# Expert layer: 16 more tokens through fetched expert rows, 368 instead of 384 through the dense product

## The reference

```
q = (xb @ w_q).reshape(T, 8, 2, 128)                       # 8 heads, two halves
s = einsum('thpd,hpkd->thpk', q, sub_keys)                 # 128 keys per half
sv, si = top_k(s, 16)
cand = sv[:, :, 0, :, None] + sv[:, :, 1, None, :]         # 16 x 16 pairs
top_s, pos = top_k(cand, 16)
eidx = the pair's index, si_0 * 128 + si_1                 # one of 16384 experts
gate = softmax(top_s)
act = gelu(einsum('thkd,td->thk', expert_u[eidx], xb))
out = einsum('thk,thkd->td', gate * act, expert_v[eidx])
```

## Time and profile before

| | |
|---|---|
| timed, median of 3 | 2393.5 us |
| profiled execution, its own time | 2388.96 us |
| its span | 2387.6 us |
| TensorE busy over the span | 2278.5 us (95%) |
| VectorE | 1777.1 us (74%) |
| ScalarE | 1095.6 us (46%) |
| GpSimd | 574.4 us (24%) |
| DMA moved | 466.79 MB, 196 GB/s on average |

### The profile page before, as it was taken

One profiled execution on the slowest core, in us unless ns is written; L12 is line 12 of the kernel. 1 busy time (PEld: TensorE's weight loads), 2 busy tenths in 40 slices (PEclk: granted clock), 3 DMA queues, 4 the chain that ended last, 5 costly groups with the idle time before them and its releaser, 6 DMA issues.

```text
span 2387.6 us, 34419 instructions
## 1 busy us (share of the span) xinstructions
PE 2278.5 (95%) x12827; PEld 2012.0 (84%) x12827; DVE 1777.1 (74%) x3434; ACT 1095.6 (46%) x1956; POOL 574.4 (24%) x419
## 2 busy tenths in 40 slices
PE   7989999999999999999999998999888899999998
PEld 5768999999999999999999997688655577777766
DVE  7889869988899976888888886633577645477764
ACT  4232343333488863333333335422366623566662
POOL 4110357888722212222222211200000020000001
PEclk9999999999999999999999999999999999999998
DMA  6546558899989999999999992111100022100012
GB/s 259 186 159 221 194 181 287 310 311 316 324 278 335 330 330 335 345 355 362 335 341 352 352 335 92 53 62 62 36 1 1 18 62 84 40 23 23 23 36 71
DMA packets 162374, 466.79 MB, mean 196 GB/s; under 512 B 15520, under 2 KB 72992, under 8 KB 159776
## 3 DMA queue, kind: packets, MB, share of 16 engines
q1 hardware_dynamic: 100512, 305.19, 36.0%
q0 software_dynamic: 36864, 134.23, 16.1%
q10 hardware_dynamic: 24832, 25.17, 3.3%
HBM read 412.10 MB, written 52.43 MB: 195 GB/s over the span
## 4 chain that ended last, share of the span: by engine, by line
PE 82%; DVE 7%; ACT 4%; issue 3%; DMA 3%; POOL 1%; SPq 0%; ACTq 0%; DVEq 0%; POOLq 0%
PE psum L491 7%; PE psum L629 7%; PE psum L492 7%; PE psum L493 7%; PE psum L631 7%; PE psum L630 7%; PE psum L482 6%; PE psum L483 6%; PE psum L484 6%; PE psum L602 4%; PE psum L509 2%; PE psum L978 2%; PE psum L795 2%; DMA arena<-hidden 2%; DVE weights_low L1536 1%
## 5 line engine op out<-in xcount | busy, mean ns | idle before, releaser
L1027 ACT ACTIVATE weights_high<-arena 128x1024 fp32r<-128x1024 f32 x355 | 374.6, 1056 | 462.5 <-PE psum L631 324.0
L1536 DVE TENSOR_TENSOR weights_low<-arena,weights_high 128x1024 fp32r<-128x1024 f32 x266 | 331.7, 1247 | 225.8 <-ACT weights_high L1027 224.6
L629 PE MATMUL psum<-hidden_high,weights_high 128*128 128x384 f32 x1024 | 344.0, 336 | 6.4 <-issue 3.7
L491 PE MATMUL psum<-x_high,weights_high 128*128 128x384 f32 x1024 | 345.8, 338 | 4.1 <-POOL weights_low L2186 2.7
L630 PE MATMUL psum<-hidden_low,weights_high 128*128 128x384 f32 x1024 | 342.7, 335 | 0.0
L631 PE MATMUL psum<-hidden_high,weights_low 128*128 128x384 f32 x1024 | 342.6, 335 | 0.0
L492 PE MATMUL psum<-x_low,weights_high 128*128 128x384 f32 x1024 | 342.2, 334 | 0.0
L493 PE MATMUL psum<-x_high,weights_low 128*128 128x384 f32 x1024 | 342.2, 334 | 0.0
L482 PE MATMUL psum<-x_high,weights_high 128*128 128x512 f32 x696 | 276.8, 398 | 14.0 <-DVE weights_low L1536 9.1
L484 PE MATMUL psum<-x_high,weights_low 128*128 128x512 f32 x696 | 272.4, 391 | 0.0
L483 PE MATMUL psum<-x_low,weights_high 128*128 128x512 f32 x696 | 272.4, 391 | 0.0
(11 more groups left out here) (263 smaller groups left out, 4294.4 us busy)
## 6 DMA issues: line engine op xcount, KB each, us to landing
arena<-in_stream SPq DMA_DIRECT2D x227, 512.0 KB, 4.6
arena<-in_v_rows SPq DMA_DIRECT2D x128, 512.0 KB, 6.4
arena<-in_ada_w SPq DMA_DIRECT2D x48, 512.0 KB, 3.5
hidden<-arena SPq DMA_DIRECT2D x128, 192.0 KB, 4.5
router<-arena SPq DMA_DIRECT2D x12, 2048.0 KB, 9.3
arena<-hidden SPq DMA_DIRECT2D x128, 192.0 KB, 6.8
arena<-router ACTq DMA_DIRECT2D x16, 1536.0 KB, 20.2
arena<-in_pair_w SPq DMA_DIRECT2D x8, 640.0 KB, 3.9
```

The lines of the kernel that those rows point to most:

```text
L491: PE.matmul(bank[b][:, 0:N], wh[w][:, k, :], xh[:, k, PICKED:T], start=k == 0, stop=False)
L629: PE.matmul(out, wh[w][:, n, :], hh[:, r, :], start=e == 0, stop=False)
L1027: ACT.activation(wh[BUFFER[u]], slots[u % RING], AF.Copy).then_inc(*tick("weights_high", u))
L1536: DVE.tensor_tensor(wl[BUFFER[u]], slots[u % RING], wh[BUFFER[u]].bitcast(F32), ALU.subtract).then_inc(*tick("weights", u))
```

## The change

Sixteen more tokens, numbers 128 to 143, leave the dense product: `DENSE` is 144 and N is 368. Their rows are fetched in another arrangement: a partition stands for one of the 16 tokens and one of its 8 heads, so that one fetch brings one of the 16 entries of each head, and 16 U rows and 16 V rows do for all of them. The tokens are copied eight times each by GpSimd (`few_copies`), turned by eight transposes and copied by ScalarE into `few_x` (SBUF). Their indices and gates are brought into this arrangement by four small DMAs through DRAM. At the end eight matmuls with a 0/1 matrix `few_sel` add the eight heads of each token.

The U rows come between the u rows of the router jobs; 85 rows are used in the jobs where 80 were, and 53 where 42 were in the scatter stage's 32 units. The stage buffers hold 16 tokens and are four, so that `router` has 23 stages, and a run of a gate load has 512 B. There are 92 quads. GpSimd makes the low weights of twelve units of the scatter stage as well (`POOL_LOWS`: units 90, 92, ... 112, of which VectorE then makes none).

```diff
-N = T - PICKED
+DENSE = PICKED + P // HEADS
+N = T - DENSE
-JOB_ROWS = [0, 0, 10, 14, 14, 14, 14, 14]
-ROW_LAG = sum(JOB_ROWS) + 6
-STAGE = 32
+FEW = P // HEADS
+FEW_FROM, FEW_SLOTS = 46, 36
+JOB_ROWS = [0, 0, 10, 15, 15, 15, 15, 15]
+ROW_LAG = sum(JOB_ROWS) - FEW + 6
+STAGE = 16
+STAGE_RING = 4
...
+POOL_LOWS = [unit("up", i) for i in range(1, KEYS) if i <= UNDER_ROUTER + 1 or i % 2 == 0 and i < 114]
...
     for n in range(ENTRIES + ROW_LAG):
+        while FEW_FROM <= len(ROWS) < FEW_FROM + FEW_SLOTS:
+            slot = len(ROWS) - FEW_FROM
+            few_u = slot * FEW // FEW_SLOTS
+            if (slot + 1) * FEW // FEW_SLOTS == few_u:
+                break
+            ROWS.append(("U", few_u))
         ROWS += [("u", n)] * (n < ENTRIES) + [("v", n - ROW_LAG)] * (n >= ROW_LAG)
+        if n - ROW_LAG >= 40 and n % 4 == 0 and few_v < FEW:
+            ROWS.append(("V", few_v))
...
-            more = 1 + (n % 3 // 2 if n < KEYS - UNDER_ROUTER - LAST_UPS else 0)
+            more = 1 + (n % 3 > 0 if n < KEYS - UNDER_ROUTER - LAST_UPS else 0)
...
+        PE.wait_ge(*at("pooled", "few"))
+        for half in range(2):
+            PE.wait_ge(*at(("q_a", "q_v")[half], 12 + half))
+            for c in range(KC // 2):
+                last = PE.transpose(bank[half][:, c * P:(c + 1) * P], few_copies[:, half * KC // 2 + c, :], K("ident"))
...
+                PE.matmul(bank[n][:, PICKED:DENSE], few_acc[:, n * P:(n + 1) * P], few_sel, start=True,
                               stop=True).then_inc(*tick("summed_down", n))
...
-            if where == 0 and half >= 2:
-                ACT.wait_ge(*at(f"g_out{half % 2}", half - 2))
+            if where == 0 and half >= STAGE_RING:
+                ACT.wait_ge(*at(f"g_out{half % STAGE_RING}", half - STAGE_RING))
...
+            if table == "U":
+                if entry == 0:
+                    DVE.wait_ge(*at("x_rows", ("few", 1)))
+                DVE.scalar_tensor_tensor(one, one, 1.0, few_x, ALU.mult, ALU.mult,
+                                         accum_out=few_act[:, entry:entry + 1]).then_inc(*tick("row_used", j))
+                return
+            if table == "V":
+                weight_of = few_w[:, entry:entry + 1]
...
+                    DVE.wait_ge(*at("scattered", QUADS - 1))
+                    DVE.tensor_scalar(few_acc, one, weight_of, None, ALU.mult).then_inc(*tick("row_used", j))
...
-            low_weights(unit("up", UNDER_ROUTER + n) + 1)
+            if unit("up", UNDER_ROUTER + n) + 1 not in POOL_LOWS:
+                low_weights(unit("up", UNDER_ROUTER + n) + 1)
...
+        POOL.wait_ge(*at("normed", ("ffn", KC - 1)))
+        POOL.tensor_copy(few_copies.rearrange("p c (t h) -> p c t h", h=HEADS),
+                         xn[:, :, PICKED:DENSE].rearrange("p c (t o) -> p c t o", o=1).to_broadcast([P, KC, FEW, HEADS])
+                         ).then_inc(*tick("pooled", "few"))
...
         for kind, n in ROW_STEPS[JOBS:]:
+            if kind == "up" and unit("up", UNDER_ROUTER + n) + 1 in POOL_LOWS:
+                low_weights(unit("up", UNDER_ROUTER + n) + 1)
             for j in ROWS_AT[kind, n]:
                 fetch_row(j + ROW_RING)
...
+            elif i == JOB_UNIT[5] + 6:
+                SP.wait_ge(*at("gated", 3))
+                SP.wait_ge(*at("few_moved", "chosen_in"))
+                load("few_moved", "gate_out", d["few"][1], gate[0:FEW, 1, :])
```

More of the change, by code:

```diff
@@ L227, in write @@
     hot0 = area(76, 16, KEYS)
-    stage = [area(24, KEYS, STAGE), area(32, KEYS, STAGE)]
+    stage = [area(24 + 4 * i, KEYS, STAGE) for i in range(STAGE_RING)]
     iota = K("iota")
@@ L1150, in scalar @@
                 *tick("x_rows", half))
+        for half in range(2):
+            ACT.wait_ge(*at("x_turned", ("few", half)))
+            ACT.activation(few_x[:, half * T:(half + 1) * T], bank[half], AF.Copy).then_inc(*tick("x_rows", ("few", half)))
         def exponents_of(job):
@@ L2179, in fetch_row, with low_weights @@
             table, entry = ROWS[j]
[L2180 to L2184 removed]
+            if (table, entry) == ("U", 0):
+                POOL.wait_ge(*at("few_moved", "chosen_in"))
+            places = few_chosen if table in "UV" else chosen
+            POOL.indirect_dma_start(rows[j % ROW_RING], None, d[f"{table.lower()}_rows"], bass.IndirectOffsetOnAxis(
+                ap=places[:, entry:entry + 1].bitcast(U32), axis=0)).then_inc(*tick(f"row{j % ROW_RING}_in", j, 16))
+        def low_weights(u):
             POOL.wait_ge(*at("weights_high", u))
@@ L2187, in gpsimd @@
                 *tick("weights_pool", u))
+        for i in range(UNDER_ROUTER + 1):
+            low_weights(unit("up", i) + 1)
             if i == JOB_UNIT[2] + 1:
@@ L2316, in low_done @@
     def low_done(u):
-        return at("weights_pool" if unit("up") < u <= unit("up", UNDER_ROUTER) + 1 else "weights", u)
+        return at("weights_pool" if u in POOL_LOWS else "weights", u)
     sync(nc.sync)
```

68 lines of the change are left out of this document (52 added, 16 removed).

## The result

The changed kernel takes 2423.3 us (median of 4, 2417.3 to 2433.2) where the kernel before takes 2393.0: 1.0128 times as long, 95% interval 1.0104 to 1.0152. It is slower by some 30 us, the forecast was 2392 with a range up to 2420. The profiled execution took 2421.91 us, 32.95 more than that of before.

What follows compares the result with a forecast made beforehand. TensorE was taken as first in router, scatter and down, each near a tie with VectorE or DMA. Terms -7.4 + 15.9 - 1.3 + 3.6 - 14.3 + 1.8 = -1.7 us, from the median 2393.5 to 2392; range 2362 to 2420.

Steps and rivals of the forecast that it cites:

- Router stage: Up units 0 to 88 with the start: VectorE ends last, its last gating comes earlier, -7.4 us.
- Of the 25.6 us of waits for rows I keep 5: Router stage: VectorE's waits for fetched rows fall from 25.6 to 5 us, a guess between none and all.
- VectorE's sum: Router stage: VectorE's busy time 229.1 + 5 x 1.21 + 11.2 (U rows stopped by GpSimd, 0.7 each) = 246.4 us.
- Scatter stage: The 32 scatter units: GpSimd's 12 low weights stop a full VectorE, 1.9 us each, 22.7 in all; stage +15.9 us.
- first rival: Scatter stage: GpSimd's low weights cost VectorE nothing, TensorE sets 210 us (-8.9); kernel 2363 us, chance 0.24.
- Last units and the start of down: Last 8 up units -1.3 us by fewer columns; first gate load longer by its 512 B runs, +3.6 us.
- Down stage: The 128 down units: the DMA sets the pace, 4.10 us a unit, 524.8 us, -14.3.
- divided by the highest share seen, 1.04: Down stage: DMA time of 4.21 us a unit over share 1.04 gives 4.05, above TensorE's 4.00.
- DMA sum: Down stage, DMA engine time per unit: fetched rows 1.57, gates 0.65, q1 with hidden rows 1.99, together 4.21 us.
- 0 at a share of 1.0: Down stage, slow bound: no gain if the DMA engines reach only share 1.0; the other bound is -26.5 us.
- slower rival: Gate loads in down: a 512 B run costs 47 ns, nearly a 1 KB run's 52; stage +20.3, kernel 2426 us, chance 0.18.
- the forecast's line through two sizes: Gate loads: a line through 52 ns for 1 KB and 179 ns for 4 KB gives 31 ns for 512 B.

Runs made afterwards that it cites:

- e2: Changed kernel, U rows multiplied with the first 128 tokens in PSUM instead of the 16 tokens' SBUF copy: 2403.1 us, 1.0048 times the kernel before.
- e6: Changed kernel with 1 KB runs, scatter low weights back on VectorE, U rows last in the router stage with a PSUM operand: 2396.0 us, 1.0024 times before.
- e7: e6 with GpSimd issuing each router-stage fetch one unit later: 2392.9 us, 1.0009 times the kernel before.
- e12: Changed kernel with only GpSimd's router-stage fetches one unit later: 2420.1 us, 1.0120 times the kernel before.
- e1: Changed kernel with all 32 low weights of the scatter stage back on VectorE: 2404.9 us, 1.0051 times the kernel before.
- e4: Changed kernel with the second gate load issued in the first down unit, some 15 us later: 2421.4 us, 1.0163 times the kernel before.
- e5: Changed kernel with two staging buffers of 32 tokens, so gate loads have 1 KB runs again: 2425.8 us, 1.0131 times the kernel before.
- e10: e7 with 42 rows in the scatter stage and the first two gate loads issued by SyncE instead of ScalarE: 2381.4 us, 0.9966 times the kernel before.
- e11: e10 with two rows instead of one fetched in each of the last units ahead of down: 2387.6 us, 0.9992 times the kernel before.
- e9: Changed kernel loading only one expert of eight from the third gate load on: 2402.8 us, 1.0042 times the kernel before.
- e3: Kernel before with four staging buffers of 16 tokens, so gate loads have 512 B runs: 2396.4 us, 1.0030 times the kernel before.
- e8: e6 with 42 rows instead of 53 in the scatter stage, the eleven others used in down: 2390.3 us, 0.9989 times the kernel before.

## Why the prediction was wrong, by its steps

**Router stage: wrong by 16.7 us, the largest miss.** The step that failed is "Of the 25.6 us of waits for rows I keep 5, ... because VectorE is now the later one and fetches pile up ahead of it". VectorE's work was right (246.4, measured 245.7); its idle time was 18.4 us, 17.1 of it for rows, and in e2, e6, e7 and e12 it waited 17 to 22 us for rows, too. Fetches can't pile up: they are four ahead at most, and each stands in GpSimd's queue among low weights that go at TensorE's pace. The step also took that queue in one direction only. A fetch that waits for VectorE holds up the low weights behind it, so VectorE's lateness reached TensorE along the way (15.1 us, 2.7 before); the sum put this at nothing. e2 shows that the U rows' stops set off most of it (-12.2 us), e7 and e12 that the queue passes it on. Which link of this loop keeps VectorE's own waits at 17 us was not separated.

Cut alike, the window took 254.7 us before and 264.1 after, +9.4 where -4.8 was forecast. Its start, 0.1 us earlier (398.35 for 398.49) and not 2.6, makes up the rest of the miss. That VectorE's sum came out is in part luck: U rows lost 0.98 us each, not 0.7, which is 4.4 us more, and the window of the earlier trace rows held 1.5 us of maxima that the same cut doesn't have; other small items made up for the rest.

**Scatter stage: right in its mechanism, in part by luck in its size.** +15.9 forecast, +17.0 measured, and e1 takes 16.4 back. The stops fell on the TENSOR_SCALARs: at the pace of before, 336 comparisons take 93.1 us (101.7 / 367 each), they took 121.4, so 28.3 us for the window's 11 low weights, 2.6 each (the forecast had 1.9, for 12). The twelfth ran at 661.75, ahead of the stage, and stopped nothing. So the stops cost 5.6 us more than the 22.7 forecast, and all the rest of the stage 3 less (208.8 where 210.9 / 0.995 was forecast). The first rival (no cost) is refuted here.

**Last units and the start of down: size off** (+2.3, measured +4.0). The mechanism behind it was another than the one forecast: not the load's bytes, but ScalarE's queue held by the issue, and behind that late stores of hidden rows (e4, e5, e10).

**Down stage: wrong by 15.1 us.** The failed step is "divided by the highest share seen, 1.04 ... so the DMA sets the pace", with 0.05 us a unit added for late hidden rows: no unit goes at such a pace. The terms of the DMA sum were near: in the 520 us the engines were busy for 0.98 of some 123.5 units, 4.13 us each, where 4.21 was forecast. But 1.04 was a 12 us burst, and time that is divided by a share says nothing of when data come late. The stage is TensorE's 127 units of 4.00 us, 508, plus 15.9 us of stops, plus 10.9 us in which TensorE was busy at less than full pace (518.9 us of busy time for 508); 13 units hold 24.6 of these 26.8 us. The forecast had 12.2 us above TensorE alone. I had "0 at a share of 1.0" as the bound and took the other end. Other runs show that the share is no ceiling either: over 520 us of the stage e11 went at 1.00 and 367 GB/s, the changed kernel at 0.98 and 352. What holds is simpler: hidden rows and gates come late with the gate loads, whose bytes e9 takes away and most of the lateness with them, and a lateness costs TensorE its stop and some slow clock behind it.

**The slower rival named the right time (2426) for the wrong reason; that is luck.** It put a run of 512 B at 47 ns. Measured, 41440 packets held 14.5% of 16 x 520 us, 29 ns each; the forecast's line through two sizes gave 31. The runs did lengthen the loads (20.2 to 25.8 us), but taking them back (e5) gave nothing, and they alone (e3) cost 0.3%. GpSimd's stops are worth 16.4 us in the scatter stage by e1 and 12.2 in the router stage by e2, about the 30 us between them, while the 26.5 us that TensorE saves in the down stage did not get through to the end.

**Left out altogether: the clock.** The sums had TensorE at 4.00 us a unit between stops; behind stops of some microseconds it worked on at half pace for a while, as at 932.74 and 1009.44. In the down stage that is the 10.9 us.

What stays open: how much of the down stage's late data the sixteen more fetched rows cause beside the gate load. e9 took away most of the gates' bytes. Rows were only moved: eleven into the stage in e8 (+1.3 us) and seven out of it in e11 (-11.0), both within what one profile of this stage leaves open.

## What to carry to other kernels

Work moved to GpSimd is not free for VectorE, even where VectorE waits for nothing of it. Beside GpSimd's subtraction of 2.40 us the TENSOR_TENSORs and SCALAR_TENSOR_TENSORs with both operands in SBUF that met it stood still (L1715, the U rows), and TENSOR_SCALARs, too: eleven subtractions that VectorE does in 1.2 us each cost it 2.6 us each when moved. When an engine's queue carries two kinds of work, a wait in one delays the other: draw the loop from the late engine through that queue back to the one that was to gain. A share of DMA time is no stock of work to be divided: ask instead which load is under way when data come late.

## What the runs showed of the hardware

Not every VectorE operation is stopped by GpSimd. From 396 to 664 us GpSimd made its 2.4 us subtractions for 147 of 268 us, and yet the changed kernel's 16 TENSOR_REDUCEs of 1024 elements in SBUF took 1207 to 1220 ns and its 32 MAX8s of 256 elements 401 to 418, also where they began inside such a subtraction. A u row with one operand in PSUM took 1191 to 1222. A U row took up to 3633 (1203 at best), and a comparison in the scatter stage up to 3160 (327 at best).

A DMA issue can take long: with 2944 runs of 512 B a load, a second load's issue on the same queue 9.2 us behind the first took 6.48 us (6.99 in e3 with 3072, 8.4 us behind), and 0.37 to 0.38 with 1536 runs of 1 KB in all 16 loads of e5, 9.9 us apart for the first two, or when it came 26.6 us later (e4). That the queue was full of the first load's runs is the reading that fits; the trace does not show the queue itself.

The DMA engines' busy share stayed at 0.96 in e9 though 18 MB of 183 were gone in a window of about as many units: the same number of packets remained, and those of the other queues took longer than in the changed kernel.
